# Hybrid decoder step: input rows and identity loaded first, constants and page table from ScalarE's queue, page and bound arithmetic behind the input's squares

## What is computed

```python
x = x + 0.5 * swiglu(x, g_ffn1, w1_gate, w1_up, w1_down)
x = x + mixer(rmsnorm(x, g_mix))      # latent attention, dilated window attention, mLSTM, HGRN2
x = x + 0.5 * swiglu(x, g_ffn2, w2_gate, w2_up, w2_down)

def swiglu(x, g, w_gate, w_up, w_down):
    h = rmsnorm(x, g)
    return (silu(h @ w_gate) * (h @ w_up)) @ w_down
```

## Time and profile before

| | us |
|---|---|
| median of 3 runs | 1827.65 |
| lowest, highest | 1826.86, 1829.4 |
| profiled execution, its own time | 1823.13 |
| span of the profiled execution | 1821.6 |
| PE busy | 1644.8 (90%) |
| DVE busy | 754.8 (41%) |
| ACT busy | 327.0 (18%) |
| POOL busy | 211.7 (12%) |

### The profile page before, as it was taken

The page is one execution under the profiler, slowest core; times in us unless marked ns, Lnnn a source line. Parts: engine busy times, 40 slices in busy tenths (PEclk is TensorE's granted clock), DMA queues, the critical chain, the costliest instruction groups (busy, mean ns, idle before and its releaser), DMA issues.

```text
span 1821.6 us, 25526 instructions
## 1 busy us (share of the span) xinstructions
PE 1644.8 (90%) x8954; PEld 1330.7 (73%) x8954; DVE 754.8 (41%) x1396; ACT 327.0 (18%) x854; POOL 211.7 (12%) x259
## 2 busy tenths in 40 slices
PE   5999999998798489999979999999988875999998
PEld 3888876667566368888868888776775653788887
DVE  3343213755457424442124441146545754344411
ACT  1000001433454200000000000024335541000000
POOL 2000000231413200000000000013313321000000
PEclk9999999998898689999989999999988986999999
DMA  6877442321621546886558765333117006588652
GB/s 227 300 251 249 129 147 96 113 76 32 213 54 33 164 149 225 293 273 165 149 183 276 231 220 140 115 132 106 47 53 235 19 27 206 185 281 264 210 138 77
DMA packets 236761, 295.16 MB, mean 162 GB/s; under 512 B 10264, under 2 KB 221384, under 8 KB 232936
## 3 DMA queue, kind: packets, MB, share of 16 engines
q1 hardware_dynamic: 228040, 197.93, 35.9%
q0 software_dynamic: 8608, 95.79, 15.0%
HBM read 287.43 MB, written 73.33 MB: 198 GB/s over the span
## 4 chain that ended last, share of the span: by engine, by line
PE 74%; issue 10%; DVE 3%; POOL 3%; ACT 3%; SPq 2%; DVEq 2%; POOLq 2%; DMA 1%; ACTq 0%
PE bank L1703 35%; PE bank L1720 17%; PE bank L1743 7%; PE bank L2102 3%; PE bank L1749 2%; PE bank L1897 2%; PE bank L2066 2%; SPq L415 2%; POOLq L619 2%; PE bank L1676 1%; PE bank L1739 1%; DMA act_T<-in_cache_swa_v 1%; PE bank L2009 1%; PE bank L1847 0%; PE bank L1746 0%
## 5 line engine op out<-in xcount | busy, mean ns | idle before, releaser
L1703 PE MATMUL bank<-h_T,ring 128*128 128x264 f32 x2816 | 633.8, 389 | 14.7 <-DVE h_T L1073 14.7
L1703 PEld LDWEIGHTS bank<-h_T,ring 128*128 128x128 f32 x2816 | 539.8, 192 | 109.0 <-DVE h_T L1073 16.7
L1720 PE MATMUL bank<-act_T,ring 128*128 128x264 f32 x1408 | 313.9, 386 | 0.0
L1720 PEld LDWEIGHTS bank<-act_T,ring 128*128 128x128 f32 x1408 | 268.0, 190 | 45.3
L1080 DVE TENSOR_SCALAR sg<-sg 128x264 f32<-128x264 f32 x88 | 26.2, 298 | 347.8 <-ACT sg L693 347.8
L1082 DVE RECIPROCAL sg<-sg 128x264 f32<-128x264 f32 x88 | 158.7, 1803 | 6.5
L1743 PE MATMUL bank<-ring,h_T 128*128 128x256 f32 (+2 forms) x512 | 156.8, 462 | 3.2 <-DVE h_T L1073 3.2
L2066 PE MATMUL bank<-wuk,TM 128*128 128x288 f32 x512 | 151.6, 444 | 0.0
L693 ACT ACTIVATE sg<-bank 128x264 f32<-128x264 f32 x88 | 34.3, 390 | 611.9 <-PE bank L1703 611.9
L1093 DVE SCALAR_TENSOR_TENSOR x_T<-bank,x_T 128x264 f32<-128x264 f32 x48 | 20.8, 433 | 297.7 <-PE bank L1720 259.3
L1743 PEld LDWEIGHTS bank<-ring,h_T 128*128 128x128 f32 x512 | 98.9, 197 | 51.6 <-issue 38.1
(11 more groups left out here) (398 smaller groups left out, 1441.9 us busy)
## 6 DMA issues: line engine op xcount, KB each, us to landing
ring<-in_w_gate SPq DMA_DIRECT2D x44, 1024.0 KB, 7.3
ring<-in_w_up SPq DMA_DIRECT2D x44, 1024.0 KB, 9.5
ring<-in_w_down SPq DMA_DIRECT2D x64, 704.0 KB, 6.2
out_s_swa_k<-in_cache_swa_k POOLq DMA_DIRECT2D x16, 2047.0 KB, 9.6
out_s_swa_v<-in_cache_swa_v POOLq DMA_DIRECT2D x16, 2047.0 KB, 14.9
ring<-in_w_in SPq DMA_DIRECT2D x16, 1024.0 KB, 6.5
ring<-in_w_in SPq DMA_DIRECT2D x16, 512.0 KB, 4.6
h_T<-in_cache_swa_k SPq DMA_DIRECT2D x48, 128.0 KB, 2.3
```

Of the source, the lines that this page charges most:

```text
L1703: last = pe.matmul(bank(2 * q + g, P, NT), w[:, g, c, q * P:(q + 1) * P], h_T[:, c, :], start=(c == 0), stop=(c == KC - 1))
L1720: last = pe.matmul(bank(4 + m % 2, P, NT), w[:, c, :], act_T[:, c, :], start=(c == 0), stop=(c == FT - 1))
```

## The change

Six things move; no arithmetic is added or taken away.

- SP's queue now holds the input rows and one more load, the identity alone (128 columns of `cst`, which is 64 KB), counted on `x_loaded`. The ring's loads follow directly.
- The page table (eight DMAs), `gcols`, `lbx`, `cbias` and the rest of the constants (3072 columns) are issued by ACT, right behind its table load and ahead of everything else that it does; the large one is the last of the twelve.
- PE's transposes wait for `x_loaded` only (now four loads). Its wait for `constants_loaded` stands ahead of the first mixer product instead, together with the wait for `TM` and `qrb`.
- DVE squares the input first; page and bound arithmetic follow.
- ACT copies the turned blocks first; the exponential for the bound follows.
- POOL's iota stands ahead of the clearing of `TM` and `qrb` instead of behind it.

```diff
@@ SP
             sp.dma_start(xin[0:DEC, 2, :], t["x_sample"].rearrange("b s d -> (b s) d")).then_inc(sem("x_loaded"), 16)
-            for j in range(RUNS):
-                sp.dma_start(pidx[j * PAGES:(j + 1) * PAGES, DEPTH, :], t["page_table"].rearrange("o (b g) -> g (o b)", b=DEC),
-                             allow_slow_non_contiguous=True).then_inc(sem("constants_loaded"), 16)
-            for dst, name in ((cst, "constants"), (gcols, "g_col"), (lbx, "lb_col"), (cbias, "c_bias")):
-                sp.dma_start(dst[:], t[name]).then_inc(sem("constants_loaded"), 16)
+            sp.dma_start(ident, t["constants"][:, K_ID:K_ID + P]).then_inc(sem("x_loaded"), 16)
@@ POOL
             pool.memset(eps[:, :], EPS).then_inc(sem("ones_set"), 1)
+            pool.iota(psub[:, :], [[0, 1]], base=0, channel_multiplier=1).then_inc(sem("iota_done"), 1)
             pool.memset(TM[:, :, :], 0.0).then_inc(sem("ones_set"), 1)
             pool.memset(qrb[:, :, :, :], 0.0).then_inc(sem("ones_set"), 1)
-            pool.iota(psub[:, :], [[0, 1]], base=0, channel_multiplier=1).then_inc(sem("iota_done"), 1)
@@ ACT
             act.preload_act_table_set("natural_log_exp_and_others")
-            act.wait_ge(sem("ones_set"), 4)
-
-            act.wait_ge(sem("lb_shifted"), 1)
-            act.activation(lbs[:, :, 0:H], lbs[:, :, H:2 * H], ACT.Exp).then_inc(sem("lb_exp"), 1)
+            for dst, name in ((gcols, "g_col"), (lbx, "lb_col"), (cbias, "c_bias")):
+                act.dma_start(dst[:], t[name]).then_inc(sem("constants_loaded"), 16)
+            for j in range(RUNS):
+                act.dma_start(pidx[j * PAGES:(j + 1) * PAGES, DEPTH, :], t["page_table"].rearrange("o (b g) -> g (o b)", b=DEC),
+                               allow_slow_non_contiguous=True).then_inc(sem("constants_loaded"), 16)
+            act.dma_start(cst[:, P:], t["constants"][:, P:]).then_inc(sem("constants_loaded"), 16)
+            act.wait_ge(sem("ones_set"), 2)
 
             for c in range(KC):
                 act.wait_ge(sem("x_turned"), c + 1)
                 act.copy(x_T[:, c, :], bank(c, P, NT)).then_inc(sem("x_copied"), 1)
+
+            act.wait_ge(sem("lb_shifted"), 1)
+            act.activation(lbs[:, :, 0:H], lbs[:, :, H:2 * H], ACT.Exp).then_inc(sem("lb_exp"), 1)
@@ DVE: the loop of the squares (L1059 to L1069 of before), whole, now stands ahead of
+            for c in range(KC):
+                dve.wait_ge(sem("x_copied"), c + 1)
+                ...
             dve.wait_ge(sem("iota_done"), 1)
             dve.tensor_scalar(psub[:, :], psub[:, :], 4, None, ALU.logical_shift_right)
             dve.wait_ge(sem("constants_loaded"), (RUNS + 4) * 16)
@@ PE
-            pe.wait_ge(sem("constants_loaded"), (RUNS + 4) * 16)
-            pe.wait_ge(sem("x_loaded"), 3 * 16)
+            pe.wait_ge(sem("x_loaded"), 4 * 16)
...
-            pe.wait_ge(sem("ones_set"), 4)
+            pe.wait_ge(sem("ones_set"), 2)
...
                 norm(l, 1)
+                pe.wait_ge(sem("ones_set"), 4)
+                pe.wait_ge(sem("constants_loaded"), (RUNS + 4) * 16)
                 pe.wait_ge(sem("small_loaded"), (l + 1) * 3 * 16)
```

More of the change, by code:

```diff
@@ L1028, in _ @@
             dve.memset(sst[:, :], 0.0).then_inc(sem("stream_out"), OUT_CREDIT)
+            for c in range(KC):
+                dve.wait_ge(sem("x_copied"), c + 1)
+                dve.drain()
+                last = dve.tensor_tensor(sqx[:, :], x_T[:, c, :], x_T[:, c, :], MUL)
+                dve.drain()
+                if c < KC - 1:
+                    some = dve.tensor_tensor(ssum[:, :], ssum[:, :], sqx[:, :], ADD)
+                if c == KC - 2:
+                    some.then_inc(sem("squares_ready"), 1)
+            last.then_inc(sem("squares_ready"), 1)
             dve.wait_ge(sem("iota_done"), 1)
@@ L1057, in _ @@
                 dve.tensor_scalar(lbs[:, i, H:2 * H], lbt[:, 0, :], -1.0, 1.0, MUL, ADD)
[L1059 to L1068, removed]
             def norm(l, k):
```

## The result

| | before | after |
|---|---|---|
| median of 20 runs, us | 1828.82 | 1823.04 |
| lowest, highest | 1820.77, 1835.88 | 1813.87, 1830.14 |
| profiled execution, its own time | 1823.13 | 1819.71 |
| span of the profiled execution | 1821.6 | 1818.2 |
| first product of the first SwiGLU, us | 30.89 | 23.74 |

The ratio is 0.9964, with a 95% interval of 0.995 to 0.9978: faster by 6.6 us of 1828.8 (4.0 to 9.1). The predicted time, 1818.2, was 4.8 us too low, and the range, 1815.5 to 1824.8, holds the measured median. The front, the stretch ahead of the first product, became 7.15 us shorter and not 9.5. The profile of the version with the bound arithmetic ahead is of a disturbed execution of 2900 us, of which only the front is read.

The account below looks back on a forecast made before the run. PE bounds three quarters; only time before the first SwiGLU product (30.89 us) can be won. Constants at 17.0 + 0.1 + 3.73 give `h_T` at 20.8, first product 21.4: 9.5 us gained, median 1818.2 us, range 1815.5 to 1824.8.

Parts of the forecast that it names:

- the one that was forecast: Constants landing at 16 to 19 us (17.0 taken), first product at 21.4 us, 9.5 us gained; chance 0.50.
- constants late: Rival: half shares or slower page table, constants landing at 19 to 26.6 us, gain 7 to 0, middle 1823.2; chance 0.20.
- The sign and the place: Faster: the front before the first SwiGLU's first product shrinks by 9.5 us, and the whole gain reaches the end.
- Input and turning: PE's transposes of the input start at 6.7 us, 8.8 us earlier, 1.5 us at most behind the identity's last bytes.
- ACT's issues: ACT's twelve DMA issues end at 7.8 us and delay the first copy of turned blocks by some 0.2 us.
- the slower rival: Both issuing engines' loads served in turn, 2.88 us per ring load: 9.0 us lost, 1836.7; chance 0.08.
- Squares: DVE's input squares, first at about 8.2 us, seven steps of 1.02 us each, eighth at 15.3 us.
- Constants: Loads on ACT's queue: 7.65 us of page table, bytes from 11.35 us, 4.1 us transfer, landing at 17.0 us.
- Arithmetic behind the squares: DVE's page and bound arithmetic and three copies, now between constants and `h_T`, add 3.73 us.
- The clearing: Rival: POOL's clearing holds DVE's squares, first product at 27.1 us, 3.8 us gained, 1823.9; chance 0.04.
- the iota: POOL's iota, put ahead of the clearing, comes at 10.2 us, 8.84 us behind `eps`, before DVE asks.

## Why the prediction was right, and where its sizes were off

- *Which case came true.* Not the one that was forecast. The constants landed at 19.59 us, outside the 16 to 19 that had a chance of 0.50 and inside the rival "constants late" (19 to 26.6, chance 0.20), by one of the two reasons given there: a page table that goes slower beside a full ring. The range held because it had been drawn to take in most of that rival. That the median lies within 0.2 us of that rival's 1823.2 is luck, since that number went with a landing at 22. Of the 4.8 us between 1818.2 and the median, 2.3 are the front; 1.2 come from the median of before, which was 1828.82 over 20 executions and not 1827.65; the rest is the difference between the front's 7.15 and the medians' 5.8, which lies inside the interval.
- *The sign and the place.* Right: PE no longer waits for the constants, the front shrinks, and its gain reaches the end of the first SwiGLU whole (7.2 us at the second root) and then the ratio (6.6 us).
- *Input and turning.* Forecast 6.7 us, measured 8.34, 7.25 and 8.63 in three profiles of the kernel after. The term took the identity's landing as undisturbed. With the ring and the page table behind and beside it, it came later; with SP alone (6.35 and 6.83) or without the single elements (7.04) it came within 0.4 us of the forecast.
- *ACT's issues.* Forecast to end at 7.8, and to cost some 0.2 us. They began 1.3 us earlier than I had them, beside the table load, but the page table took 5.86 us and not 3.65, so they ended at 9.14. The first copy followed at 9.33 and the first square at 9.80, against 8.2. In this profile the first block is turned at about 9.2 as well, so both delays end together; in the second profile it is turned a microsecond earlier, and the first copy still starts at 9.32, behind the issues. So this term was mis-sized for the squares, though the first product did not feel it, since the squares ended before the constants were there. I had weighed an issue that is held by the other queue only as the slower rival, at its full price of 2.88 us each; what happens is about 0.3 us for each of the eight.
- *Squares.* 1.02 us each, as forecast; the eighth at 16.93, later by what the first was later.
- *Constants.* Forecast at 17.0, measured at 19.59. Their transfer by the packets' lengths was right (92% of the engines' share against one packet each). Its start was wrong: by the step that carried 7.65 us of page table over to ACT's queue, as if no other queue were at work, the bytes should have begun at 11.35; they began in the stretch 13 to 14. This is the step of the forecast that failed.
- *Arithmetic behind the squares.* 3.73 us forecast, 3.60 measured (19.59 to 23.19). With 2.6 us from the constants' landing, this makes the first product 23.7 instead of 21.4, the whole miss of the front.
- *The clearing.* The rival that it holds DVE's squares is refuted by the trace: 0.43 us each beside it. The rule of the Trainium skill ("SBUF — State Buffer", Who interferes with whom), two SBUF inputs against an instruction that only writes, agrees. But I had asked about the wrong instructions. The same section says that `copy` and `tensor_scalar` can run in a mode that takes both ports and that one side then blocks fully. The runs agree for the first such operation beside a clearing: 7.00 and 5.65 us for a copy, 1.70 and 1.79 us for the two `pidx` operations. The shift of `psub`, a scalar operation on one column, was not held (0.15 us), and no run shows why. In the kernel after this hold cost nothing, only because the clearing ended at 19.37 us, 0.2 us ahead of the constants; the iota ahead of it had come at 12.39 and not at 10.2, where I had it.

## What to carry to other kernels

Put ahead of the first product only what it needs, and give each later load a semaphore of its own: one count over all constants cost the first product 1.9 us here. When a wait is taken away, follow the arithmetic that stood behind it; its new place (2.3 us slower or 7 us faster) decided the sign. And put a long clearing on POOL where DVE has nothing to do, since moving it by a few us made a copy of 0.2 us take 7.

## What the runs showed of the hardware that was not expected

- A POOL memset of 6.9 us held a DVE copy until its end (7.00 us for one that takes 0.18), even a copy of four columns (5.65 us), and the scalar operations on `pidx` (1.70 and 1.79 us). It left alone squares and sums with two SBUF operands (0.43 us), a reduction and a reciprocal (0.16 and 0.18 us), and a scalar operation on one int32 column (0.15 us).
- Eight loads of 128 single elements on one queue nearly stop the other as well: 3, 46 and 19 GB/s in 6 to 7 us in three profiles, against 293 GB/s with runs of eight elements.
- The iota's delay of issue is no constant: 8.84 us in the kernel before, and 9.02 to 11.60 in the others.
